# Transposes of both inversion streams taken in one step of a two-way interleave

## The reference, cut to what matters

```
def step(S, inp):
    r_t, w_t, k_t, v_t, nkk_t, b_t = inp
    sa = jnp.einsum('bhvk,bhk->bhv', S, nkk_t)
    S = S * w_t[:, :, None, :] + sa[..., None] * b_t[:, :, None, :] + v_t[..., None] * k_t[:, :, None, :]
    return S, jnp.einsum('bhvk,bhk->bhv', S, r_t)
S_final, ys = lax.scan(step, state0, xs, reverse=reverse)
```

## Time and profile before

| | us |
|---|---|
| median of three runs | 3926.23 (3924.54 to 3931.3) |
| the profiled execution, its own time | 3932.56 |
| its span, first to last instruction | 3930.7 |
| PE busy in the span | 3705.4 |
| PE busy in the 432 us from 748 to 1180 | 358.02 |

### The profile page before, as it was taken

How to read it: one execution, slowest core, us unless ns; L and a number is a source line. 1 busy time by engine, 2 the same in 40 slices (tenths; PEclk the granted TensorE clock), 3 DMA queues, 4 the chain that set the end, 5 groups by cost and what they waited for, 6 DMA issues and landing times.

```text
span 3930.7 us, 73718 instructions
## 1 busy us (share of the span) xinstructions
PE 3705.4 (94%) x31436; PEld 3212.8 (82%) x31436; DVE 1978.0 (50%) x2442; ACT 1647.0 (42%) x2118; POOL 1387.5 (35%) x631
## 2 busy tenths in 40 slices
PE   8988999888888999999998999998899999999998
PEld 5767888777757788888887888887788888888887
DVE  3268867566536785444445544336333344343443
ACT  3433226533324444443444444434344444444443
POOL 3232222000004454454544445444344333334342
PEclk9999999999988999999999999999999999999999
DMA  8886763000004576555554555454555555555543
GB/s 302 305 305 242 286 225 103 24 4 4 15 22 165 185 263 225 184 193 190 187 173 159 173 180 169 161 176 150 177 180 174 172 172 169 182 170 177 172 167 128
DMA packets 183380, 669.09 MB, mean 170 GB/s; under 512 B 20464, under 2 KB 20464, under 8 KB 182416
## 3 DMA queue, kind: packets, MB, share of 16 engines
q1 hardware_dynamic: 176688, 643.12, 48.5%
q10 hardware_dynamic: 5088, 17.07, 1.2%
q0 software_dynamic: 1280, 4.20, 0.3%
HBM read 655.92 MB, written 8.39 MB: 169 GB/s over the span
## 4 chain that ended last, share of the span: by engine, by line
PE 78%; DVE 11%; ACT 4%; issue 3%; DMA 2%; PEld 2%; POOL 1%; ACTq 0%; DVEq 0%; PEldq 0%; SPq 0%; POOLq 0%
PE ps L1054 64%; DVE whl L2046 3%; ACT whl L1541 2%; DVE raw L2130 2%; PEld ps L1054 1%; PE ps L1281 1%; PE ps L1294 1%; DVE tm L2049 1%; DMA raw<-in_mem 1%; PE ps L1210 1%; PE ps L1529 1%; PE ps L1272 1%; PE ps L1513 1%; ACT work L1541 1%; DVE halves L2049 1%
## 5 line engine op out<-in xcount | busy, mean ns | idle before, releaser
L1054 PE MATMUL ps<-halves,whl 128*128 128x256 f32 (+1 forms) x14752 | 2590.1, 336 | 85.0 <-DVE halves L2046 23.6
L1054 PEld LDWEIGHTS ps<-halves,whl 128*128 128x128 f32 x14752 | 2245.2, 191 | 399.5 <-issue 90.2
L2653 POOL TENSOR_TENSOR whl<-raw,whl 128x1024 fp32r<-128x1024 f32 x508 | 1259.6, 2480 | 1783.7 <-ACT whl L1541 1783.5
L1541 ACT ACTIVATE whl<-raw 128x1024 fp32r<-128x1024 f32 x1016 | 1057.3, 1053 | 951.0 <-PE ps L1054 689.0
L2046 DVE TENSOR_TENSOR whl<-raw,whl 128x1024 fp32r<-128x1024 f32 x508 | 794.7, 1565 | 1141.8 <-ACT whl L1541 1141.5
L1054 PE MATMUL ps<-whl,halves 128*128 128x256 f32 x2752 | 488.5, 336 | 14.3 <-POOL whl L2653 10.8
L1054 PEld LDWEIGHTS ps<-whl,halves 128*128 128x128 f32 x2752 | 417.7, 189 | 75.2 <-ACT whl L1541 12.7
L1541 ACT ACTIVATE work<-ps 128x512 f32<-128x512 f32 (+1 forms) x208 | 119.0, 575 | 302.7 <-PE ps L1054 249.0
L2130 DVE SCALAR_TENSOR_TENSOR raw<-raw,mix 128x1024 f32<-128x1024 f32 x128 | 226.1, 1790 | 3.9 <-DMA raw<-in_adaT 3.7
L2653 POOL TENSOR_TENSOR halves<-mix,halves 128x256 fp32r<-128x256 f32 (+1 forms) x15 | 25.7, 1716 | 505.4 <-ACT halves L1541 505.4
L2046 DVE TENSOR_TENSOR work<-work,ps 128x512 f32<-128x512 f32 x157 | 107.5, 684 | 110.8 <-ACT work L1541 109.9
(11 more groups left out here) (258 smaller groups left out, 2433.6 us busy)
## 6 DMA issues: line engine op xcount, KB each, us to landing
raw<-in_ffn SPq DMA_DIRECT2D x264, 512.0 KB, 4.4
raw<-in_w_kv SPq DMA_DIRECT2D x192, 512.0 KB, 3.7
raw<-in_w_in_b SPq DMA_DIRECT2D x160, 512.0 KB, 3.9
raw<-in_adaT SPq DMA_DIRECT2D x128, 512.0 KB, 5.2
raw<-in_w_in_a SPq DMA_DIRECT2D x128, 512.0 KB, 3.8
raw<-in_ada SPq DMA_DIRECT2D x64, 512.0 KB, 6.0
raw<-in_mem SPq DMA_DIRECT2D x64, 512.0 KB, 5.1
raw<-in_w_out_a SPq DMA_DIRECT2D x48, 512.0 KB, 3.6
```

What stands on the lines that cost most here:

```text
L1054: p = self.e.matmul(o, x, y, start=bi not in begun, stop=final and kc == 3 and m == len(pairs) - 1, skip_group_check=True)
L1541: return self.e.activation(out, in_, func, **kw)
L2653: return self.e.tensor_tensor(out, a, b, op)
```

## The change

Two `yield`s of `invert` leave the loops over the streams. Before, each stream's transposes were a step of their own, so an inversion had 2 + 5 x 6 = 32 steps and took 16 rounds. Now the transposes of both streams are one step: 1 + 5 x 5 = 26 steps, 13 rounds. No instruction is added or removed, and no tile or wait changes.

```
     def invert(self, n):
         for s in range(2):
             self.inv_xt(n, 0, s)
-            yield
+        yield
         for lv in range(1, 6):
             for s in range(2):
                 self.inv_t1(n, lv, s)
...
             for s in range(2):
                 self.inv_xt(n, lv, s)
-                yield
+            yield
```

## The result

The changed kernel takes 3965.69 us, the median of five runs (3960.71 to 3969.24), against 3926.23 (3924.54 to 3933.58): the medians differ by 39.5 us. The ratio over all the runs is 1.0096, with a 95% interval of 1.0084 to 1.0108. The forecast was 3949, slower by 23, in a range that ended at 3970.

What follows compares the result with a forecast made beforehand. The recurrence was held bound by PE's work plus the latency of PE to DVE or ACT and back. 0.4 + 2 x 2.8 + 2 x 4.5 + 2 x 3 + 2 = +23 on 3926.2 gave 3949 us, range 3922 to 3970.

Steps and rivals of the forecast that it cites:

- The pairing as the cause: Recurrence: only the pairing changes; three of five rounds hold a stage and its own successor, and the transposes' neighbourhood brings nothing.
- Round 6: Chunk 1: T1 of s0 waits for the copy standing behind ACT's 2.97 us of decay; wait of 2.8 us.
- Rounds 7 and 8: Chunk 1: x of s1 waits 2.3 us for its mask behind Z's two, Xt of s1 2.4 behind kd.
- The sum of waits: Recurrence and the first inversion: PE's new waits, priced by chunk, add up to +23 us.
- The walk: Round-by-round count of old and new order at the same prices; for chunk 1 it gave 42.7 and 45.5 us.
- The clock: Rival: one more slow stretch in each of chunks 0 to 5, +10 more, +33 in all, 3959 us; chance 0.17.
- The first inversion: invert(0) beside prepare(1): walk from lw to av 40.05 us against 39.63 in the trace, +0.4, ends -3 and +3.
- Chunks 0 to 5: Periods of the recurrence: +2.8 each for chunks 0 and 1, +4.5 for 2 and 3, +3 for 4 and 5.
- Bare steps: Ends of chunks 2 and 3: four woven steps without inversion instead of one, bound by DVE; walk +5.5, taken as +4.5 each.
- the sign: For the bare steps: the new trace would show waits of L1210 and L1305 for DVE at chunk ends.
- Chunk 6: Bonus after the inversion: six bare turns instead of five, one more +2.6, shorter inversion against it; +2, ends -2 and +5.
- Faster: Rival: x and Xt of s1 find inputs within 1 us and the old 3.00 us wait goes; -10, 3916 us, chance 0.12.

Runs made afterwards that it cites:

- The split as such: Kernel before, with one step for both streams' transposes at level 0 only, from the second inversion on: 3941.01 us, ratio 1.003.
- The fillers: Changed kernel, with 204 transposes of the identity that nobody reads put on TensorE ahead of four waits: 3948.01 us, ratio 1.0052.
- the two late starts: Inversion begun some rounds late, to end with the chunk: in the changed kernel 3968.84 us, in the kernel before 3930.36 us.

## Why the prediction was right, and where its sum was off

- **The pairing as the cause.** Right. The transposes stood together before, their neighbourhood brought nothing, and the loss came with stages that stand behind their own releasers and with split halves. The split as such is measured (13.6 us); the share of the tight rounds is what is left over.
- **Round 6, T1 behind ACT's decay, 2.8 us.** The sum written out there gives 2.7. It was 1.66 in chunk 1, with transposes that took 1.97 in place of 1.09 in front of it, so part of the wait was filled by slower work. Moving 1.15 us of ACT's copies cut these waits by 8.6 us in sum, which shows the step.
- **Rounds 7 and 8, 2.3 and 2.4.** Round 7's sum gives 2.2. They were 1.90 and 1.87, with the releasers that were named. The waits for X rose to 15.8 us where "10 and more" stood.
- **The sum of waits.** The walk's +23 was built of waits alone, and idle time rose by 19.3. This term was right in size. By the windows, from chunk 0 to chunk 6, idle time rose by 2.3, 4.4, 4.9, 2.4, 2.6, 1.6 and 1.5 us against 2.8, 2.8, 4.5, 4.5, 3, 3 and 2.
- **The clock.** This is the term that was mis-sized: it stood in the sum at nothing and as a rival of +10 with a chance of 0.17. It was not a rival but the other half, 22 us of longer products beside the waits. The fillers took 17.7 us back. The rival as it was written, the forecast and the clock added up to 23 + 10 = +33, should have been the centre. What is left to 39.5 has about the size of the miss in the first inversion. The measured time lies within the range because the range took in this rival; the forecast's own sum is 16.5 us short.
- **The first inversion, +0.4.** Wrong. The window grew by 6.6 us, and the change there alone cost 8.3. PE's idle time in it did not rise, 7.0 us against 7.5, though it has a single wait of 3.04; its busy time rose by 7.1, at a clock of 0.78 in place of 0.96. A walk at the full clock could not see this.
- **Chunks 0 to 5.** By the windows +3.7, +6.2, +6.6, +4.0, +6.0 and +6.5 against 2.8, 2.8, 4.5, 4.5, 3 and 3. For chunks 4 and 5 I held that gaps named "issue" would swallow part of the walk's 4.9 us of waits. In sum the waits were indeed fewer: idle time rose by 2.6 and 1.6. What I left out is the clock, which had been 0.97 and 1.00 there and fell to 0.91 in both: PE's busy time rose by 3.4 and 4.9.
- **Bare steps.** The extra for chunks 2 and 3 was put on them. PE's waits of L1210 and L1305 for DVE came as the sign asked, but small: 5.5 us in the whole recurrence where they were 1.8. Chunks 2 and 3 gained hardly more idle time (4.9 and 2.4) than chunks 0 and 1 (2.3 and 4.4), and the two late starts won nothing, so the size of this step isn't borne out.
- **Chunk 6, +2.** The window grew by 1.7, and six bare turns stand where five stood. But the agreement is in part luck: five traces with this chunk in the old order have 66.5 to 71.0 us for it, four with the changed order 69.5 to 73.2, and the means are 3.7 apart.
- **Faster.** Its point of decision, inputs within 1 us, wasn't reached: 1.90 and 1.87. The old 3.00 us wait was worth removing all the same, but by DVE's order alone, with nothing split: 7.6 us.

## What to carry to other kernels

In an interleave written by hand, the step between a stage and its successor is what hides the latency. Fewer and fuller rounds save nothing if a stage then stands behind its own releaser, and to split the halves of a stage over two rounds cost some 14 us here by itself. Price a new wait on TensorE twice, once as idle time and once as the products behind it at half the clock, above all where the clock is full now. And look first at the order of the engine that serves: here one swap on DVE and some unread work on TensorE gave 18.7 us, while every change of the rounds that was tried cost time or won nothing.

## What the runs showed of the hardware that was not expected

Work that nobody reads made kernels faster: 17.7 us in the changed kernel, 5.1 in the one before, and in the bonus 1.05 us a turn. The granted clock was higher with it each time, 1.00 in the bonus. The length of a wait doesn't tell how much slow time follows. With its 3.04 us wait the first inversion of the changed kernel has some 20 us at the lower clock ((1 - 0.78) x 2 x 46.21), and with its 3.00 us wait chunk 1 of the kernel before has some 6 ((1 - 0.93) x 2 x 43.73), both by estimate. And the bonus in chunk 6 stayed at the lower clock, 0.50 from 1142 to 1162 us, through turns whose only pause is 0.7 us each. And one profiled execution of a kernel whose loss is in the clock may stand several us from the median of its runs, as with kd ahead of Z in the changed kernel (its own time 3960.47, median 3964.85).
